# A decoder trunk in split fp32: the array of activations moves from below the weight buffers to behind the constants in SBUF

## What is computed

```python
def reference(x, norm_g, even_w_in, even_w_out, ..., ffn_w_up, ffn_conv_w, ffn_conv_b, ffn_w_down):
    h = x                                                # (1, 256, 1024)
    for layer in range(2):
        y = rmsnorm(h, norm_g[layer, 0])
        y = even_mixer(y, ...) if layer % 2 == 0 else odd_mixer(y, ...)
        h = h + rmsnorm(y, norm_g[layer, 1])
        y = conv_ffn(rmsnorm(h, norm_g[layer, 2]), ...)  # 1024 -> 2 x 2816 -> conv, gelu gate -> 1024
        h = h + rmsnorm(y, norm_g[layer, 3])
    return h
```

## Time and profile before

| | us |
|---|---|
| median of 3 runs | 689.08 |
| lowest and highest | 687.07, 690.55 |
| the profiled execution, whole | 689.5 |
| its span, first to last instruction | 687.5 |
| TensorE busy in it | 668.7 (97%) |
| VectorE, ScalarE, GpSimd busy | 459.3, 380.4, 154.0 |
| granted TensorE clock | 0.999 of full speed |

### The profile page before, as it was taken

How to read it: one execution, slowest core, us unless ns; L and a number is a source line. 1 busy time by engine, 2 the same in 40 slices (tenths; PEclk the granted TensorE clock), 3 DMA queues, 4 the chain that set the end, 5 groups by cost and what they waited for, 6 DMA issues and landing times.

```text
span 687.5 us, 10253 instructions
## 1 busy us (share of the span) xinstructions
PE 668.7 (97%) x3719; PEld 560.3 (82%) x3719; DVE 459.3 (67%) x620; ACT 380.4 (55%) x539; POOL 154.0 (22%) x117
## 2 busy tenths in 40 slices
PE   4999999999999999999999999999999999999996
PEld 3888887778788888888887999777788888888885
DVE  4596775577776878786547563576676878786532
ACT  5556435476476666767334634375475757676320
POOL 0021220000122434343001000372113343444000
PEclk9999999999999999999999999999999999999999
DMA  8957643001365353544752745301545353634601
GB/s 337 400 200 268 220 161 122 1 2 62 123 215 213 131 236 131 235 147 182 292 189 109 274 159 237 127 1 53 193 160 211 148 225 141 236 130 184 245 0 61
DMA packets 18651, 116.20 MB, mean 169 GB/s; under 512 B 2463, under 2 KB 3133, under 8 KB 5693
## 3 DMA queue, kind: packets, MB, share of 16 engines
q1 hardware_dynamic: 17325, 111.52, 43.3%
q10 hardware_dynamic: 1296, 4.26, 1.8%
HBM read 114.72 MB, written 1.05 MB: 168 GB/s over the span
## 4 chain that ended last, share of the span: by engine, by line
PE 92%; DVE 2%; ACT 2%; issue 2%; POOL 1%; DMA 1%; DVEq 0%; POOLq 0%
PE ps L1516 22%; PE ps L1155 13%; PE ps L1157 13%; PE ps L1156 13%; PE ps L1518 11%; PE ps L1197 5%; PE ps L1351 3%; PE ps L1277 1%; PE ps L1311 1%; PE ps L1150 1%; PE ps L1567 1%; PE ps L1437 1%; PE ps L1556 1%; PE ps L1287 1%; POOL rstd L1070 1%
## 5 line engine op out<-in xcount | busy, mean ns | idle before, releaser
L629 DVE TENSOR_TENSOR wlo<-raw,whi 128x2048 fp32r<-128x2048 f32 x99 | 226.0, 2311 | 69.6 <-ACT whi L333 69.5
L1516 PE MATMUL ps<-xpair,whi 128*128 128x512 f32 x640 | 226.4, 399 | 0.0
L333 ACT CAST whi<-raw 128x2048 fp32r<-128x2048 f32 x99 | 186.1, 1916 | 71.2 <-PE ps L1157 66.8
L1518 PE MATMUL ps<-xpair,wlo 128*128 128x256 f32 x640 | 179.8, 281 | 0.0
L1516 PEld LDWEIGHTS ps<-xpair,whi 128*128 128x128 f32 x640 | 120.3, 188 | 29.9
L1518 PEld LDWEIGHTS ps<-xpair,wlo 128*128 128x128 f32 x640 | 120.9, 189 | 0.0
L1110 POOL TENSOR_TENSOR hidf<-act_g,conv 128x512 f32<-128x512 f32 x22 | 74.6, 3392 | 83.9 <-ACT act_g L533 83.9
L1157 PE MATMUL ps<-whi,hid_lo 128*128 128x512 f32 x176 | 69.4, 395 | 0.0
L1156 PE MATMUL ps<-wlo,hid_hi 128*128 128x512 f32 x176 | 69.4, 394 | 0.0
L1155 PE MATMUL ps<-whi,hid_hi 128*128 128x512 f32 x176 | 69.4, 394 | 0.0
L1155 PE MATMUL ps<-whi,xpair 128*128 128x512 f32 x168 | 67.2, 400 | 0.2
(11 more groups left out here) (174 smaller groups left out, 987.5 us busy)
## 6 DMA issues: line engine op xcount, KB each, us to landing
raw<-in_weights SPq DMA_DIRECT2D x101, 1024.0 KB, 4.9
c_gpre<-in_gpre ACTq DMA_DIRECT2D x4, 512.0 KB, 4.7
raw<-in_weights SPq DMA_DIRECT2D x4, 512.0 KB, 8.5
c_gpost<-in_gpost ACTq DMA_DIRECT2D x4, 512.0 KB, 4.9
h<-in_x SPq DMA_DIRECT2D x2, 512.0 KB, 7.7
out<-h SPq DMA_DIRECT2D x4, 256.0 KB, 2.0
t<-in_masks SPq DMA_DIRECT2D x1, 512.0 KB, 14.1
c_rope<-in_rope SPq DMA_DIRECT2D x1, 256.0 KB, 14.0
```

The costliest lines, as they stand in the source:

```text
L333: act.copy(whi[:, slot, :], raw[:, slot, :]).then_inc(hi_done, 1)
L629: dve.tensor_tensor(wlo[:, slot, :], raw[:, slot, :], whi[:, slot, :].bitcast(F32), ALU.subtract).then_inc(lo_done, 1)
L1516: pe.matmul(ps[:, b0 + m, :], whi[:, slot, cols], xpair[:, kt].rearrange("p a c -> p (a c)"), start=kt == 0, stop=kt == KT - 1, skip_group ...
L1518: ins = pe.matmul(ps[:, b0 + m, 0:SEQ], wlo[:, slot, cols], xhi[:, kt, :], start=False, stop=kt == KT - 1, skip_group_check=True)
```

## The change

`xpair` is asked for after the constants and ahead of the stage buffers. Nothing else is edited: no instruction is added, removed or moved to another place, and no wait is changed.

```diff
         h = sb("h", [P, TT, D])
         xn = sb("xn", [P, TT, D])
-        xpair = sb("xpair", [P, KT, 2, SEQ], F32R)
-        xhi, xlo = xpair[:, :, 0, :], xpair[:, :, 1, :]
         raw = sb("raw", [P, RING, UNIT])
         whi = sb("whi", [P, RING, UNIT], F32R)
         wlo = sb("wlo", [P, RING, UNIT], F32R)
...
         rstd = sb("rstd", [P, 2, TT])
         mhalf = sb("mhalf", [P, 1])
 
+
+        xpair = sb("xpair", [P, KT, 2, SEQ], F32R)
+        xhi, xlo = xpair[:, :, 0, :], xpair[:, :, 1, :]
 
         a = ctx.enter_context(ExitStack())
         vbuf = sb("vbuf", [P, TT, 1280], F32, a)
```

## The result

The changed kernel takes 690.24 us, the median of 20 runs (690.04 to 691.97), against 689.26 us for the kernel before in the same session (20 runs, 687.07 to 690.87). The ratio is 1.002, with a 95% interval of 1.0012 to 1.0028: slower by 0.2%, clear of noise but well under 0.5%. The profiled execution takes 690.45 us, its span 688.4 against 687.5.

The account below looks back on a forecast made before the run. TensorE, busy 668.7 of 687.5 us, was taken as the bound. The terms +2.8 + 1.3 + 0 = +4.1 us on the profiled 689.5 gave 693.6, or 693.2 against the median, with an 8-in-10 range of 685.5 to 697.5.

Parts of the forecast that it names:

- The reading of the two rates: Output projection at 226.7 ns, down projection at 232.3: operands starting alike modulo 512 settle into the short step, others don't.
- The first term: Stages with stationary `xpair` and moving weights: 498 of 696 steps lose the settled 226.7 ns, 5.7 ns each, +2.8 us.
- The second term: `channel_blocks`, moving `xpair`, 256 columns: 384 settled 120.0 ns steps become unsettled, +1.3 us.
- the price for losing a settled run: In `channel_blocks`: 3.3 ns a step, from the up projection's 353.3 ns a pair against a settled 346.7.
- The third term: Up projection, 640 pairs: already unsettled, so no change, 0 us, with bounds -4.3 and +3.1.
- The rival in which the up projection gains: Up projection finds a shorter step with unlike starts: 687.6 us at 346.7 ns a pair, 683.4 at 340; chance 0.18.
- its point of decision, 348.9 ns: Up projection: a pair must fall below this from 353.3 ns for the whole kernel to gain at all.
- the main case: Stationary stages and the 256-column stage unsettle, up projection stays: 693.2 us, own range 691.5 to 694.5, chance 0.34.
- Nothing moves: Rival: operand reads are independent and the down projection is slower for another reason; 689.1 us, chance 0.16.
- Only the stationary operand's start counts: Rival: only the stages with stationary `xpair` slow, +2.8 us, giving 691.9 us; chance 0.22.

Follow-up runs that it names:

- s1: Kernel before with 256 unused bytes between `xpair` and the ring and 128 ahead of the stage buffers: 687.83 us, ratio 0.9969.
- s2: Kernel before with 128 unused bytes between `xpair` and the ring and 256 ahead of the stage buffers: 690.26 us, ratio 1.0006.
- e1: Changed kernel with 384 unused bytes ahead of `xpair` and 128 behind, restoring its old start modulo 512: 689.51 us, ratio 1.000.
- s3: Kernel before, padded so the ring starts 32 bytes below `xpair`'s remainder and the hidden activations 160 above the ring's: 687.42 us, ratio 0.9973.
- s4: Kernel before, padded so the ring starts 64 bytes below `xpair`'s remainder and the hidden activations 192 above the ring's: 690.04 us, ratio 1.0006.
- e3: Kernel before, padded so `xpair`, ring and hidden activations all start 256 above a multiple of 512: 686.30 us, ratio 0.9944.
- e4: Kernel before with 384 unused bytes ahead of the stage buffers only, giving the hidden activations the ring's remainder: 686.48 us, ratio 0.9953.
- f1: Changed kernel with 128 unused bytes ahead of `xpair`, putting it and the hidden activations on the ring's remainder: 686.58 us, ratio 0.9948.
- g16: Kernel before with hidden activations at the ring's remainder and up-projection matmuls grouped sixteen `whi`, then sixteen `wlo`: 683.63 us, ratio 0.9901.
- e2: Kernel before with `xpair` still below the ring but starting 128 bytes higher, all else keeping its remainder: 690.48 us, ratio 1.001.

## Why the prediction was right and wrong

**The reading of the two rates**, from one contrast between the earlier trace rows, was right in all that mattered: the offset of the two operands, not load, code or place. The period was given as 512 bytes. For the stationary stages it is 256: s1 with 256 between the operands behaves as 0, and s2 with 384 as 128.

**The first term**, stationary `xpair`: forecast +2.8 us, measured +2.60, in the way named and down to the thirteen-step pattern.

**The second term**, `channel_blocks`: forecast +1.3 us, measured +0.01. The stage does lose its even step: the distances are 123, 117 and 120 ns in turn where they were 120. But their mean is the same. The step that failed is the price for losing a settled run, taken from the up projection's 3.3 ns over a sum of settled steps; that figure isn't the price of an offset, since e1 has the same loop with the same offset at 346.7. At 256 columns the uneven run was no dearer, 120.0 ns a step; s3 and s4 made it cheaper still, 116.7 and 117.8.

**The third term**, the up projection: forecast 0, measured -1.41 us, 351.1 ns a pair for 353.3. The step that failed is "a run that isn't settled has no settled step to lose". It repeats a pattern of uneven steps, and the mean of that pattern depends on the offset: 351.1 ns a pair at 128, 346.7 at 32, and at 0 either 353.3 or 346.7. The prediction named this as its largest lever and the one it knew least of, gave the bounds -4.3 and +3.1, and then put the value on zero. The rival in which the up projection gains had its sign right, and its point of decision, 348.9 ns, wasn't reached.

**The sum**: 2.6 + 0.0 - 1.4 = +1.2, less 0.2 in all other matmuls, against +4.1 forecast. The time, 690.24, lies within the range of 685.5 to 697.5 and below the main case's own range of 691.5 to 694.5. Slower was forecast and it is slower, by a quarter of what was said, which puts it within 0.5%. The reading of the rates earned the direction; the size was wrong by the second and third terms, each 1.3 to 1.4 us too high.

**Nothing moves** fell: e3, e4 and f1 change addresses alone and gain 0.5% (686.30, 686.48 and 686.58 us against 689.60 to 689.65). So the addresses of the two operands do matter to the time here. By what mechanism, these runs don't show. **Only the stationary operand's start counts** fell by e3.

Left open: the mechanism; why offset 32 suits the up projection; what decides, at offset 0, whether an FFN runs at 346.7 or 353.3 ns. Each offset was tried in one or a few placements, and none that isn't a multiple of 32 bytes; no run combines an offset of 32 for the up projection with 0 for the stationary stages.

## What to carry to other kernels

In a TensorE-bound kernel, look at the distances between matmul starts, not at durations alone: the same shape at two rates in two stages is a finding. Here tensors that meet as stationary and moving operands took 2.5% less per 512-column matmul when their SBUF starts were equal modulo 256 bytes than when they were 128 apart, and in the changed kernel an unused tensor of 128 bytes was enough to get there. Grouping equal shapes is worth a trial where the operands are aligned: sixteen by sixteen it took the up projection from 226.3 to 222.8 us, and with the pad this kernel went from 689.58 to 683.63 us. But the ungrouped loop at an offset of 32 took 222.1, so try offsets too. And a change of the order of tensors can shift every alignment behind it, so print the addresses before and after.

## What the runs showed of the hardware

- A 512-column matmul with its own 128-column weight load, its operands declared float32r, took 226.7 ns a turn at a clock of 1.00 with equal starts modulo 256 bytes, and 228.9 to 233.3 ns at the other offsets tried (32, 64, 128, 160 and 192). After a change of width it took five matmuls to reach the short turn (g16), after a pause up to 13, mostly five to ten (the kernel before, e3, e4, f1).
- At 256 columns the turn was 120.0 ns with equal starts and 116.7 with an offset of 32: there the equal start is not the best.
- Executions of one kernel differed by 2.1 us with nothing changed, by the rate at which one FFN's loop happened to run (579 or 568 matmuls in 100 us), and by some 1.8 us more where a stretch of 3.4 us had a granted clock of 0.50 (e2 at 451.4 us, 692.24 against 690.48; g16 at 446.5, 684.59 against 682.67 and 682.82). Each looks like an effect of the addresses in a median of few runs; the distances by stage and the mean clock of each execution tell them apart.
